# Dense part of V at 992 columns, every second block in three passes of rounded halves, five places for gathered rows

## The chip, the cores and the metric

One core of a Trainium2 chip runs the whole program in one launch. The metric is the device time of that core in microseconds (us), lower is better. The engines are PE (matmuls), ScalarE (ACT), VectorE (DVE), GpSimd (POOL, which here mostly issues gathers by index) and SyncE (SP, which issues plain loads and stores); 16 DMA engines serve all queues.

## The reference, cut to what matters

The program is one transformer layer for 256 tokens of width 2048: a mixer of several attentions, then a "PEER" layer of 16,384 experts. Only the last part of the second is touched. In it each token has 8 heads x 16 picked experts; each pick has a number `expert_idx`, made of two keys of 128 (`a * 128 + b`), and a weight `g * act`:

```
u = expert_u[expert_idx]                       # (tokens, 8, 16, 2048)
act = gelu(einsum('chkd,cd->chk', u, x))
vv = expert_v[expert_idx]
out = einsum('chk,chkd->cd', g * act, vv)      # sum over 128 picks of each token
```

All inputs and outputs are float32. The output is x plus the mixer plus this sum.

## The kernel before

**Two halves of V.** The sum over picks is made in two ways, split by columns. The first `V_ROW` = 1152 columns of each picked row are *gathered*: a pick (one of 256 = 2 tiles of 128 tokens x 128 picks; the kernel numbers them k) fetches one row of V for each of 128 tokens by an indirect DMA that POOL issues (`v_gather`, L671; 128 x 1152 floats, 576 KB), and its weighted row is added either by VectorE (`v_add`, L1597) or by PE with a diagonal of weights (`pick_add`, L2095). The last `V_DENSE` = 896 columns are *dense*: all 16,384 rows of V are read in 128 blocks of 128 rows (L598, SP's queue, 448 KB each), and PE multiplies each block with a 128 x 128 matrix of weights for each tile of tokens (`dense`, L2127). These weight matrices `dense_w` (tile 0 in `dense0`, tile 1 in `dense1`) are nearly all zeros, 128 picks for each token among 16,384; they are built from products of one-hot rows (`group`, L2118).

**The stages.** Up to some 440 us PE multiplies the mixer's inputs and outputs in three passes of rounded halves (L1692 to L1694): ScalarE copies a 1024-column piece into `split_hi` as F32R (L719), VectorE subtracts it to get `split_lo` (L1030), and hi x hi, hi x lo and lo x hi are added up. Then VectorE takes 256 products of gathered rows of U (L1549; POOL gathers them at L691), to about 1200 us; in this stage the first `V_BESIDE` = 36 rows of V are gathered and added by PE, into three places. Then comes the *seam* (1200 to 1280 us): 32 groups of four tokens build the weights of tile 1 (VectorE L1582, ScalarE L956 and L961, PE L2118), and 37 further rows of V are gathered and added, 21 by VectorE, 16 by PE, in the order `SEAM`. The last seam rows are k = 70 (VectorE), 71 and 72 (PE). Then comes the *dense stage*: PE does the 128 blocks, VectorE adds the remaining 183 rows (k from `V_AFTER` = 73 to 255).

**What sets the order in the dense stage.** Every queue runs in program order. SP issues the load of block a when block a - 4 is done on PE (`DENSE_PLACES` = 4, semaphore `dense_used`); the loads of blocks 1 to 3 wait for the last group of the seam, since the one-hot rows lie in their places. POOL issues gather k when the row that had its place (`v_place`, `v_before`) has been added; there are `V_PLACES` = 7 places, taken in turn. VectorE adds rows in the order of k, each addition waiting for the one before, and once, at k = 80, adds PE's share into tile 0 (`tile_out`, L1604). The last row is added in two halves (L1593), then the dense results are added from PSUM (L1665) as SP stores them (L602, L606). Nothing couples the rows to the blocks, except the DMA engines.

## Time and profile before

| | |
|---|---|
| median of 3 runs | 1690.85 us (1689.32 to 1690.89) |
| the profiled execution's own time | 1694.34 us |
| its span | 1692.5 us |
| PE busy | 1234.9 us (73%) |
| DVE busy | 1298.5 us (77%) |
| ACT busy | 460.9 us (27%) |
| POOL busy | 842.8 us (50%) |
| moved by DMA | 575.81 MB, mean 340 GB/s |

Busy times are of one profiled execution, in which PE's weight loads are counted apart. In rows of the profile `L671` is line 671 of the kernel, `xN` the number of instructions, and behind the bar stand busy us, mean ns of one, and the idle time of the engine before them with what ended it. A float32 matmul is recorded as two instructions. A matmul's recorded length contains its way through the array, so the distance of two starts, not the length, says how long PE is taken.

### The profile page before, as it was taken

The numbers are of one execution on the slowest core, as the hardware profiler recorded it, in microseconds if no ns is written. First come the engines' busy times: TensorE is split into PE (matmuls) and PEld (weight loads), VectorE is DVE, ScalarE is ACT, GpSimd is POOL, SyncE is SP. The second block draws the span as 40 slices with busy tenths as digits, with TensorE's granted clock in tenths as the row PEclk, the third lists the DMA queues.
The fourth block names the chain that finished last, engine by engine and source line by source line (L and its number), as shares of the span: only waits on it lengthen the run. The fifth ranks groups of instructions, "written<-read, shape, count | busy, mean of one in ns | idle before, by whom it ended". The sixth has DMA issues, their size and how long they took to land.

```text
span 1692.5 us, 14464 instructions
## 1 busy us (share of the span) xinstructions
PE 1234.9 (73%) x4812; PEld 839.8 (50%) x4812; DVE 1298.5 (77%) x1802; ACT 460.9 (27%) x1023; POOL 842.8 (50%) x546
## 2 busy tenths in 40 slices
PE   9999999999995554001344544454699999999993
PEld 7888887778984343000122322332365555555551
DVE  5554666466699999999999999999796665666667
ACT  5333443554200100000135565552381000000000
POOL 1000010000174888877888888888565443444444
PEclk9999999999997778555666676666699999999997
DMA  8886546348799999999999999999899999999998
GB/s 237 223 207 196 169 143 213 99 148 278 260 410 415 422 411 396 385 371 362 395 382 407 403 413 387 398 401 422 335 313 380 410 409 411 410 410 409 410 409 347
DMA packets 150230, 575.81 MB, mean 340 GB/s; under 512 B 15586, under 2 KB 28596, under 8 KB 117268
## 3 DMA queue, kind: packets, MB, share of 16 engines
q0 software_dynamic: 74384, 421.30, 62.6%
q1 hardware_dynamic: 75460, 152.82, 26.9%
q8 instruction: 35, 0.57, 0.1%
q10 hardware_dynamic: 320, 0.86, 0.1%
q14 instruction: 31, 0.25, 0.0%
HBM read 572.57 MB, written 2.36 MB: 340 GB/s over the span
## 4 chain that ended last, share of the span: by engine, by line
PE 30%; DVE 28%; DMA 24%; POOL 12%; issue 4%; ACT 2%; DVEq 0%; ACTq 0%; POOLq 0%
DMA v_rows<-in_peer_expert_v,pick_row 21%; DVE big L1549 10%; DVE more_rows L1549 8%; PE ps L1692 6%; PE ps L1694 6%; PE ps L1693 6%; POOL big L691 5%; PE ps L2095 4%; POOL more_rows L691 3%; DVE big L1597 3%; POOL v_rows L671 3%; DMA more_rows<-in_peer_expert_u,pick_row 2%; PE ps L2118 1%; DMA big<-in_peer_expert_u,pick_row 1%; DVE big L1574 1%
## 5 line engine op out<-in xcount | busy, mean ns | idle before, releaser
L671 POOL DMA_INDIRECT v_rows<-in_peer_expert_v,pick_row x256 | 307.8, 1202 | 271.7 <-DVE big L1597 234.9
L1597 DVE SCALAR_TENSOR_TENSOR big<-v_rows,pick_w,big 128x1152 f32<-128x1152 f32 x203 | 287.6, 1417 | 151.7 <-DMA v_rows<-in_peer_expert_v,pick_row 149.7
L2095 PE MATMUL ps<-v_rows,diag 128*128 128x512 f32 (+1 forms) x312 | 182.9, 746 | 269.5 <-DMA v_rows<-in_peer_expert_v,pick_row 169.8
L1549 DVE CUSTOM_DVE_ANT_0 big<-big 128x2048 f32<-128x2048 f32 x150 | 340.1, 2283 | 12.9 <-DMA big<-in_peer_expert_u,pick_row 12.5
L691 POOL DMA_INDIRECT big<-in_peer_expert_u,pick_row x150 | 288.8, 1925 | 65.6 <-issue 43.2
L2095 PEld LDWEIGHTS ps<-v_rows,diag 128*128 128x128 f32 x312 | 83.3, 285 | 368.2 <-issue 194.8
L691 POOL DMA_INDIRECT more_rows<-in_peer_expert_u,pick_row x106 | 222.7, 2101 | 75.3 <-issue 28.3
L1030 DVE TENSOR_TENSOR split_lo<-raw,split_hi 128x1024 fp32r<-128x1024 f32 x119 | 145.8, 1225 | 143.7 <-ACT split_hi L719 118.1
L1549 DVE CUSTOM_DVE_ANT_0 more_rows<-more_rows,big 128x2048 f32<-128x2048 f32 x106 | 240.8, 2284 | 11.0 <-DMA more_rows<-in_peer_expert_u,pick_row 11.0
L2127 PE MATMUL ps<-big,dense 128*128 128x512 f32 (+1 forms) x512 | 213.5, 539 | 0.3 <-DMA big<-in_peer_expert_v 0.3
L2127 PE MATMUL ps<-big 128*128 128x512 f32 (+1 forms) x512 | 213.4, 539 | 0.0
L1692 PE MATMUL ps<-split_hi,ht 128*128 128x512 f32 x476 | 189.3, 398 | 1.1 <-DVE split_lo L1080 0.9
L1694 PE MATMUL ps<-split_hi,ht 128*128 128x512 f32 x476 | 185.9, 390 | 0.0
L1693 PE MATMUL ps<-split_lo,ht 128*128 128x512 f32 x476 | 185.7, 390 | 0.0
L634 POOL TENSOR_TENSOR small<-small 128x2 f32<-128x2 f32 (+4 forms) x8 | 12.7, 1592 | 329.3 <-DVE small L1228 95.4
L2127 PEld LDWEIGHTS ps<-big,dense 128*128 128x128 f32 x512 | 97.1, 190 | 95.7 <-issue 61.2
L2127 PEld LDWEIGHTS ps<-big 128*128 128x128 f32 x512 | 97.3, 190 | 95.1 <-issue 61.2
L719 ACT ACTIVATE split_hi<-raw 128x1024 fp32r<-128x1024 f32 x97 | 102.9, 1060 | 148.9 <-PE ps L1694 148.1
L2118 PE MATMUL ps<-big 128*128 128x128 f32 x512 | 83.8, 324 | 50.5 <-ACT big L948 49.6
L1007 ACT ACTIVATE big<-ps 128x512 f32<-128x512 f32 x1 | 0.6, 598 | 388.0 <-PE ps L2127 388.0
L2118 PEld LDWEIGHTS ps<-big 128*128 128x128 f32 x512 | 78.5, 238 | 53.8 <-issue 50.9
L1692 PEld LDWEIGHTS ps<-split_hi,ht 128*128 128x128 f32 x476 | 89.4, 188 | 27.6 <-issue 3.2
(281 smaller groups left out, 1495.2 us busy)
## 6 DMA issues: line engine op xcount, KB each, us to landing
big<-in_peer_expert_v SPq DMA_DIRECT2D x128, 448.0 KB, 6.8
raw<-in_w_in SPq DMA_DIRECT2D x88, 512.0 KB, 3.7
raw<-in_w_out SPq DMA_DIRECT2D x32, 512.0 KB, 5.1
big<-in_peer_w_query SPq DMA_DIRECT2D x16, 512.0 KB, 6.5
raw<-in_peer_w_query SPq DMA_DIRECT2D x8, 512.0 KB, 7.6
spare<-in_peer_w_query SPq DMA_DIRECT2D x8, 512.0 KB, 8.3
v_rows<-in_peer_expert_v,pick_row POOLq DMA_INDIRECT x256, 14.2
big<-in_peer_expert_u,pick_row POOLq DMA_INDIRECT x150, 9.1
```

What stands on the lines that cost most here:

```text
L671: pool.indirect_dma_start(v_row(k), None, v_table, bass.IndirectOffsetOnAxis(pick_row[:, k:k + 1], 0)).then_inc(v_gathered[v_place(k)], 16)
L691: pool.indirect_dma_start(ring[u_place(m)], None, u_table, bass.IndirectOffsetOnAxis(pick_row[:, m:m + 1], 0)).then_inc(gathered[u_place(m ...
L719: act.activation(split_hi[:, s % SPLIT, :], raw[:, s % RAW, :], ACT.Copy).then_inc(hi_done, 1)
L1030: dve.tensor_tensor(split_lo[:, slot % SPLIT, 0:width], raw[:, slot, 0:width], split_hi[:, slot % SPLIT, 0:width].bitcast(F32), ALU.subtra ...
L1549: dve.tensor_tensor_reduce(row, row, XN[:, place_of(m // TOPK)[0], :], 1.0, 0.0, ALU.mult, ALU.add, pick_dot[:, m:m + 1]).then_inc(dotted, 1)
L1597: dve.scalar_tensor_tensor(out=v, in0=row, scalar=pick_w[:, k:k + 1], in1=v, op0=ALU.mult, op1=ALU.add).then_inc(added, 1)
L1692: pe.matmul(acc[t], h_h, w_h, start=k == 0, stop=False)
L1693: pe.matmul(acc[t], h_h, w_l, start=False, stop=False)
L1694: ins = pe.matmul(acc[t], h_l, w_h, start=False, stop=k == KC - 1)
L2095: ins = pe.matmul(psf[:, c:c + w], diag[:, j % DIAGS, :], row[:, c:c + w], start=k == 0, stop=j == pe_adds(PICKS) - 1)
L2118: pe.matmul(ps[:, 3 + i % 2, j * P:(j + 1) * P], hot[:, 1, :], hot[:, 0, :], start=True, stop=True).then_inc(token_made, 1)
L2127: ins = pe.matmul(psf[:, o:o + w], dense_w[t][:, a, :], row[:, c:c + w], start=a == 0, stop=a == NKEYS - 1, skip_group_check=True)
```

## The change

`V_ROW` becomes 1056 and so `V_DENSE` 992. Of the 128 blocks, those with an odd number from 5 on (62 of them, `SPLIT_BLOCKS`) are multiplied in three passes of rounded halves: hi x hi, hi x lo (the row's rest), lo (the weights' rest) x hi, where all blocks went in plain float32. For such a block a:

- ScalarE, once the block has landed and PE is done with block a - 4, copies the 992 columns into `dense_hi` (two places, laid over the last two of the seven places for gathered rows) and both 128 x 128 weight matrices into the slots of block a - 4, as F32R.
- VectorE subtracts: the row's rest goes into the block's own place, the weights' rest into their own slots. Its three subtractions stand in its program between additions of rows, at row 73 + (a - 2) * 183 // 128.
- PE waits for both before the block.

From row 73 on there are five places (`V_LATE`). ScalarE's first half waits until the rows of the seam are added. The store of tile 0's gathered columns, issued by ScalarE, is now behind block 63. Four waits on semaphores with names of their own became the engine's own step counter (`link`, `step`); the order of the instructions is the same.

```diff
-V_ROW = 1152
+V_ROW = 1056
 V_DENSE = D - V_ROW
 V_FIRST_PLACES, V_PLACES = 3, 7
+HI_PLACES, HI_BEHIND = 2, 4
+V_LATE = 5
+SPLIT_BLOCKS = [a for a in range(HI_BEHIND, NKEYS) if a % 2]
+SPLIT_AHEAD = 2
+OUT_0_AT = 63
+def split_after(n):
+    return [a for a in SPLIT_BLOCKS if max(0, a - SPLIT_AHEAD) * (PICKS - V_AFTER) // NKEYS == n]
 def v_place(k):
-    return k % V_FIRST_PLACES if k < V_BESIDE else (k - V_BESIDE) % V_PLACES
+    return k % V_FIRST_PLACES if k < V_BESIDE else (k - V_BESIDE) % V_PLACES if k < V_AFTER else (k - V_AFTER) % V_LATE
...
+        at_rows = at_big[0] - DENSE_PLACES * V_DENSE
+        dense_lo = nc.alloc_sbuf_tensor_at("dense_lo", [P, DENSE_PLACES, V_DENSE], F32R, offset=at_sbuf["big"] + 4 * at_rows)
+        split_w = [nc.alloc_sbuf_tensor_at(f"split_w{t}", [P, NKEYS, P], F32R, offset=at_sbuf["big"] + 4 * (A_PROJ if t else A_X1T)) for t in range(TT)]
+        dense_hi = nc.alloc_sbuf_tensor_at("dense_hi", [P, HI_PLACES, V_DENSE], F32R, offset=at_sbuf["ht"])
...
             group_out(1, GROUPS - 1)
-            act.wait_ge(sem("out_ready"), 1)
-            act.wait_ge(added, dve_adds(TILE_PICKS))
-            act.dma_start(out_rows[:, 0, 0:V_ROW], X[:, 0, 0:V_ROW]).then_inc(out_stored, 16)
+            act.wait_ge(group_moved, TT * GROUPS)
+            act.wait_ge(added, dve_adds(V_AFTER))
+            act.wait_ge(pe_added, pe_adds(V_AFTER))
+            for r, a in enumerate(SPLIT_BLOCKS):
+                act.wait_ge(dense_loaded[a % DENSE_PLACES], 16 * (a // DENSE_PLACES + 1))
+                act.wait_ge(dense_used, a - HI_BEHIND + 1)
+                act.activation(dense_hi[:, r % HI_PLACES, :], dense_rows[:, a % DENSE_PLACES, :], ACT.Copy).then_inc(dense_high, 1)
+                for t in range(TT):
+                    ins = act.activation(split_w[t][:, a - HI_BEHIND, :], dense_w[t][:, a, :], ACT.Copy)
+                ins.then_inc(dense_high, 1)
+                if a == OUT_0_AT:
...
+            def split_low(a):
+                r = SPLIT_BLOCKS.index(a)
+                dve.wait_ge(dense_high, 2 * r + 1)
+                dve.tensor_tensor(dense_lo[:, a % DENSE_PLACES, :], dense_rows[:, a % DENSE_PLACES, :],
+                                  dense_hi[:, r % HI_PLACES, :].bitcast(F32), ALU.subtract).then_inc(dense_split, 1)
+                dve.wait_ge(dense_high, 2 * r + 2)
+                for t in range(TT):
+                    ins = dve.tensor_tensor(split_w[t][:, a, :], dense_w[t][:, a, :], split_w[t][:, a - HI_BEHIND, :].bitcast(F32), ALU.subtract)
+                ins.then_inc(dense_split, 1)
             for k in range(V_AFTER, PICKS):
+                for a in split_after(k - V_AFTER):
+                    split_low(a)
...
             def dense(a):
+                if a in SPLIT_BLOCKS:
+                    r = SPLIT_BLOCKS.index(a)
+                    pe.wait_ge(dense_split, 2 * r + 2)
+                    hi, low = dense_hi[:, r % HI_PLACES, :], dense_lo[:, a % DENSE_PLACES, :]
+                    for t in range(TT):
+                        w_hi, w_low = split_w[t][:, a - HI_BEHIND, :], split_w[t][:, a, :]
+                        for w, row in ((w_hi, hi), (w_hi, low), (w_low, hi)):
+                            for c in range(0, V_DENSE, CHUNK):
+                                o, n = DENSE_AT[t] + c, min(CHUNK, V_DENSE - c)
+                                last = a == NKEYS - 1 and w is w_low
+                                ins = pe.matmul(psf[:, o:o + n], w, row[:, c:c + n], start=False, stop=last, skip_group_check=True)
+                    ins.then_inc(dense_used, 1)
+                    return
```

## Rows read from the trace of the kernel before

**Rows 1.** The page, part 2: busy share of the DMA engines, 40 slices.

```profile
DMA  8886546348799999999999999999899999999998
```

**Rows 2.** Stretches: PE, PEld, DVE, ACT, POOL, clock, DMA share, GB/s.

```profile
1300.00:1340.00 40.00, 40.00 (x108) 20.21 (x107) 24.83 (x18) 0.00 (x0) 16.49 (x18) 1.00 1.03 410
1660.00:1692.00 32.00, 6.43 (x18) 2.97 (x16) 26.81 (x21) 0.60 (x1) 14.88 (x12) 0.66 0.85 332
```

**Rows 3.** DMA view, 1300 to 1660 us: queues, and loads to landing.

```profile
q0 software_dynamic: 22404, 91.78, 63.3%
q1 hardware_dynamic: 17250, 55.00, 38.8%
...
big<-in_peer_expert_v SPq DMA_DIRECT2D x118, 448.0 KB, 6.8
v_rows<-in_peer_expert_v,pick_row POOLq DMA_INDIRECT x156, 14.4
```

**Rows 4.** Groups by shape, 1280 to 1692 us: VectorE's additions.

```profile
L1597 DVE SCALAR_TENSOR_TENSOR big<-v_rows,pick_w,big 128x1152 f32<-128x1152 f32 x180 | 255.3, 1418 | 149.9 <-DMA v_rows<-in_peer_expert_v,pick_row 148.1
...
L1593 DVE SCALAR_TENSOR_TENSOR big<-v_rows,pick_w,big 128x576 f32<-128x576 f32 x2 | 1.5, 814 | 0.1
...
L1665 DVE TENSOR_TENSOR big<-big,ps 128x896 f32<-128x896 f32 x1 | 1.1, 1078 | 0.0
...
L1665 DVE TENSOR_TENSOR big<-big,ps 128x384 f32<-128x384 f32 x1 | 0.5, 546 | 0.0
```

**Rows 5.** Timeline of VectorE, the end of the span.

```profile
1661.68 24.25 DVE L1597 SCALAR_TENSOR_TENSOR big<-v_rows,pick_w,big 128x1152 f32<-128x1152 f32 x16 [0.57 <-DMA v_rows<-in_peer_expert_v,pick_row]
1686.03 1.54 DVE L1593 SCALAR_TENSOR_TENSOR big<-v_rows,pick_w,big 128x576 f32<-128x576 f32 x2
```

**Rows 6.** Groups by shape, POOL, 770 to 1196 us: the gathers there.

```profile
L691 POOL DMA_INDIRECT big<-in_peer_expert_u,pick_row x94 | 187.9, 1999 | 31.4 <-issue 28.0 <-DVE pick_dot L1549 3.3
L691 POOL DMA_INDIRECT more_rows<-in_peer_expert_u,pick_row x48 | 97.7, 2035 | 14.6 <-issue 14.6
L671 POOL DMA_INDIRECT v_rows<-in_peer_expert_v,pick_row x37 | 84.2, 2274 | 11.3 <-issue 11.0 <-PE ps L2095 0.3
```

**Rows 7.** Timeline of PE: the last gathered row, the first block.

```profile
1278.00 2.17 PE L2095 MATMUL ps<-v_rows,diag 128*128 128x512 f32 x6 [0.17 <-ACT diag L917]
1280.01 1.67 PE L2127 MATMUL ps<-big,dense 128*128 128x512 f32 x4
```

**Rows 8.** Timeline of POOL there: the gather that PE releases.

```profile
1280.44 1.20 POOL L671 DMA_INDIRECT v_rows<-in_peer_expert_v,pick_row  x1 [0.32 <-PE ps L2095]
```

**Rows 9.** Timeline of PE, 1401 to 1405 us: two block starts.

```profile
1401.68 1.67 PE L2127 MATMUL ps<-big,dense 128*128 128x512 f32 x4
...
1404.68 1.67 PE L2127 MATMUL ps<-big,dense 128*128 128x512 f32 x4
```

**Rows 10.** Timeline of PE, 200 us: two rounded matmuls.

```profile
200.21 0.39 PE L1692 MATMUL ps<-split_hi,ht 128*128 128x512 f32 x1
200.44 0.39 PE L1693 MATMUL ps<-split_lo,ht 128*128 128x512 f32 x1
```

**Rows 11.** Groups by shape, 60 to 500 us: making rounded halves.

```profile
L1030 DVE TENSOR_TENSOR split_lo<-raw,split_hi 128x1024 fp32r<-128x1024 f32 x102 | 124.9, 1225 | 124.7 <-ACT split_hi L719 99.0 <-ACT split_hi L773 25.3
L719 ACT ACTIVATE split_hi<-raw 128x1024 fp32r<-128x1024 f32 x80 | 84.8, 1060 | 124.3 <-PE ps L1694 123.6 <-DMA raw<-in_w_out 0.8
```

**Rows 12.** Timeline of ACT, 1267 us: four copies of 128 columns.

```profile
1266.99 1.27 ACT L956 ACTIVATE big<-big,picks_t 128x128 f32<-128x128 f32 x4
```

**Rows 13.** Timeline of SP: the load behind that block start.

```profile
1401.87 0.33 SPq L598 DMA_DIRECT2D big<-in_peer_expert_v  x1
```

**Rows 14.** Line L598 over the whole span: issue to landing.

```profile
DMA to landing us min/median/max: 3.6/6.8/10.8
```

**Rows 15.** DMA view, 60 to 250 us: loads while DMA has room.

```profile
raw<-in_w_in SPq DMA_DIRECT2D x63, 512.0 KB, 3.6
```

**Rows 16.** DMA view, 770 to 1196 us: gathered rows of V.

```profile
v_rows<-in_peer_expert_v,pick_row POOLq DMA_INDIRECT x37, 8.7
```

More of the change, by code:

```diff
@@ L386, in layer @@
         assert A_XN <= at_big[0] - DENSE_PLACES * V_DENSE and at_big[0] <= A_X1T
+        at_rows = at_big[0] - DENSE_PLACES * V_DENSE
+        dense_lo = nc.alloc_sbuf_tensor_at("dense_lo", [P, DENSE_PLACES, V_DENSE], F32R, offset=at_sbuf["big"] + 4 * at_rows)
+        split_w = [nc.alloc_sbuf_tensor_at(f"split_w{t}", [P, NKEYS, P], F32R, offset=at_sbuf["big"] + 4 * (A_PROJ if t else A_X1T)) for t in range(TT)]
+        dense_hi = nc.alloc_sbuf_tensor_at("dense_hi", [P, HI_PLACES, V_DENSE], F32R, offset=at_sbuf["ht"])
+        assert HI_PLACES * V_DENSE + V_LATE * V_ROW <= OLD_HT * D
         hot0 = ring_rest.rearrange("p (s j n) -> p s j n", s=2, j=GROUP_TOKENS)
@@ L414, in layer @@
         query_used = sem("query_used")
+        dense_high, dense_split = sem("dense_high"), sem("dense_split")
         def query_name(n):
@@ L940, in hot_first @@
                     v = hot0[:, 1, j, :]
-                    act.activation(v, iota[:, :], ACT.Square, bias=picks_t[:, 1, token:token + 1], scale=-1.0).then_inc(sem("hot_squared"), 1)
-                    act.wait_ge(sem("hot_squared"), token + 1)
+                    link(act.activation(v, iota[:, :], ACT.Square, bias=picks_t[:, 1, token:token + 1], scale=-1.0))
                     act.activation(v, v, ACT.Relu, bias=1.0, scale=-1.0).then_inc(sem("hot_act"), 1)
@@ L1001, in _ @@
             group_out(1, GROUPS - 1)
-            act.wait_ge(sem("out_ready"), 1)
-            act.wait_ge(added, dve_adds(TILE_PICKS))
-            act.dma_start(out_rows[:, 0, 0:V_ROW], X[:, 0, 0:V_ROW]).then_inc(out_stored, 16)
+            act.wait_ge(group_moved, TT * GROUPS)
[9 more added lines that the diff above has]
+                if a == OUT_0_AT:
+                    act.wait_ge(sem("out_ready"), 1)
+                    act.wait_ge(added, dve_adds(TILE_PICKS))
+                    act.dma_start(out_rows[:, 0, 0:V_ROW], X[:, 0, 0:V_ROW]).then_inc(out_stored, 16)
             act.wait_ge(dense_used, NKEYS)
             v = slice(V_ROW, V_ROW + CHUNK)
-            act.activation(X[:, 1, v], ps[:, 6, :], ACT.Copy).then_inc(sem("dense_copied"), 1)
-            act.wait_ge(sem("dense_copied"), 1)
+            link(act.activation(X[:, 1, v], ps[:, 6, :], ACT.Copy))
             act.dma_start(out_rows[:, 1, v], X[:, 1, v]).then_inc(out_stored, 16)
@@ L1554, in head_weights @@
                 dve.wait_ge(sem("head_acted"), n + 1)
-                dve.wait_ge(sem("exp_inverse"), n + 1)
                 dve.scalar_tensor_tensor(out=pick_w[:, v], in0=pick_exp[:, v], scalar=exp_sum[:, n:n + 1], in1=pick_act[:, v],
@@ L1560, in weigh @@
                 dve.wait_ge(sem("head_exp"), n + 1)
-                dve.reciprocal(exp_sum[:, n:n + 1], exp_sum[:, n:n + 1]).then_inc(sem("exp_inverse"), 1)
+                link(dve.reciprocal(exp_sum[:, n:n + 1], exp_sum[:, n:n + 1]))
                 head_weights(n)
@@ L1625, in _ @@
             after()
-            dve.tensor_tensor(pick_exp[:, 0:TOPK], head_best, head_best[:, 0:1].broadcast_to([P, TOPK]), ALU.subtract).then_inc(sem("first_exp"), 1)
+            step(dve.tensor_tensor(pick_exp[:, 0:TOPK], head_best, head_best[:, 0:1].broadcast_to([P, TOPK]), ALU.subtract))
             first_rows(1, TOPK)
-            dve.wait_ge(sem("first_exp"), 1)
+            after()
             dve.wait_ge(sem("first_rows"), 2)
```

## The prediction

> **What bounds the kernel now.** I read the page's slices first: from about 460 us to the end the DMA engines stand at 8 or 9 tenths throughout [rows 1]. So I asked of each stage whether bytes set its length. In the dense stage they nearly do: between 1300 and 1340 us the share is 1.03 at 410 GB/s, but PE is also busy for 40.00 of 40 us, while VectorE has room (24.83) [rows 2]. The DMA view splits this into the gathers (63.3%) and the blocks (38.8%) [rows 3]: per MB, 0.69 and 0.71 points, so both cost by their bytes. A gathered row takes 14.4 us to land, a block 6.8 us. VectorE waits 148.1 us there for rows [rows 4]. PE is done by 1667 us (6.43 us busy from 1660 on [rows 2]); the last 16 whole rows go through VectorE back to back in 24.25 us, and the last row's halves begin at 1686.03, 6.5 us before the end of the span [rows 5]. Two things run side by side: PE with 128 blocks, and rows that wait for bytes and end some 20 us later.
>
> **The bytes.** A row shrinks by 96 x 4 x 128 = 49,152 bytes, a block grows by as much. 256 rows less 128 blocks give 6.3 MB less, 15.3 us at 410 GB/s. That is the ceiling. It has to be divided by stage.
>
> *Beside U* (36 rows, 1.77 MB, 4.4 us at 400 GB/s). POOL's gathers there fill the stretch: 187.9 + 97.7 + 84.2 us busy and 57.3 us of idle time around them make 427 of 426 us [rows 6]. A smaller row does not shorten an issue. Bounds 0 and 4.4 us saved; I take 1.5, nearer to POOL's rows.
>
> *Seam* (37 rows). VectorE, ScalarE and PE go in step here, and PE goes from its last pick_add straight into the first block [rows 7]. A row costs VectorE 0.1 us less, but PE still has the same number of matmuls and weight loads. I take nothing; bounds 0 and 21 x 0.1 = 2.1 us saved. PE then begins block 0 at 1278.5 instead of 1280.0.
>
> *The change to five places.* Gather 79 now waits for row 72, which PE frees, and is issued at 1280.44 [rows 8]. With five places that release belongs to gather 74. So at the start of the stage five rows fewer are under way, and 182 rows (98.4 MB) and 127 blocks (64.5 MB) are still to come: 162.9 MB or 397 us, where before 177 rows and 127 blocks made 162.7 MB. This is what the places cost: hardly a byte is saved in the dense stage itself. The first split is due behind row 76 and before block 5, some 17 us after the start, when these rows are there; so it delays nothing by itself.
>
> **PE.** Two starts of a block lie 3.00 us apart for 2 x 896 columns [rows 9]; 992 make 3.32. A rounded matmul of 512 columns takes 0.23 us from start to start [rows 10], one of 480 by the same rate 0.21: six of each are 2.64 us. A pair of one plain and one split block is 5.96 us, against 6.00 for two blocks before. PE alone gains 2 us in all.
>
> **VectorE and ScalarE.** The two lengths of the addition, 1418 and 814 ns [rows 4], give 1.05 ns a column, 1.32 us for 1056; back to back one takes 24.25 / 16 = 1.52 us, 0.10 more than its length [rows 5], so 1.42. Per pair of blocks there are 183 / 64 = 2.86 rows, 4.05 us. A split adds one subtraction of 992 columns: 1225 ns for 1024 columns [rows 11] and 1078 for 896 [rows 4] give 1.18 us; and two of 128, which the line through 1078 and 546 ns puts at 0.28 each, some 0.2 from start to start. Sum 5.65 us per pair. ScalarE's copy takes 1060 ns for 1024 columns [rows 11], 1.03 for 992, and its small ones 0.3 each [rows 12]; it was idle. The store on its queue moves, and nobody waits for it before the end. SP's and POOL's queues get no instruction more.
>
> **The chain that is new.** Before, a landed block was ready. Now the load of a split block is followed by ScalarE, VectorE and then PE, and the load still goes out only when block a - 4 is done. Steps from the start of block a - 3: SP issues 0.19 us later [rows 9, 13]; landing L; ScalarE 1.03; VectorE 1.18 and 0.45; four hand-overs at 0.1 us (my allowance, from the 0.10 above). That is L + 3.2 us. PE reaches block a after one plain, one split and one plain block, 9.3 us. L was 6.8 in the median, 3.6 to 10.8 overall [rows 14]. For 508 KB it lies between 3.6, the time of 512 KB where the DMA engines had room [rows 15], and 6.8 x 992 / 896 = 7.5. I take 6.8, since the competing rows shrink as the block grows. The chain then makes 10.0 us, 0.7 more than PE has. As two pairs T fit into the chain and the split block before it: T = (L + 3.2 + 2.64) / 2, that is 6.32 us at 6.8, under PE's 5.96 at 3.6, and 6.7 at 7.5.
>
> The DMA floor of a pair is two blocks and 2.86 rows, 2.56 MB at 410 GB/s: 6.25 us. VectorE's is 5.65, PE's 5.96. With four limits inside a tenth, and a landing time that scatters, the mean lies above the largest; I take **T = 6.4**. What is queued behind VectorE's wait for ScalarE is the next rows, and with them POOL's gathers; behind PE's wait are the next blocks and so SP's loads. So rows and blocks now march together.
>
> **The end.** After the last split five rows remain. The last row's halves start 4 x 1.42 us after the split; from there 6.6 us to the end, as before [rows 5] with 0.1 for wider results. From the last split 12.3 us, from PE's end 12.3 - 2.64 = 9.65 us.
>
> **Sum.** 1278.5 + 0.9 (x1 added on PE) + 4 x 3.32 + 62 x 6.4 + 9.65 = 1699.1 us of span, 6.6 above 1692.5. The profiled execution itself took 1694.34 and the median of the runs is 1690.85; I carry the difference over: **1697.4 us**. Waits that only changed their semaphore cost nothing: the same engine waits for the same instruction.
>
> **Rivals.** About 0.2% (3.4 us) can be told from no change.
>
> *A. Bytes decide after all (faster).* If landing falls to 6.6 us or less because fewer rows are in the queue, T is the DMA floor 6.25: 1689.8 of span. With all 4.4 us beside U it is 1686.9, with the 2.1 of the seam 1684.8. Times 1683 to 1688. For it: the share of 1.03, and 14.4 us of landing show a deep row queue that will be shallower. Against: PE and the chain sit right beside it.
>
> *B. Blocks cost more than their bytes.* A block's rows now begin 4224 bytes into a row of V, no multiple of 256; if fetches go by whole pieces of 256 they cost as 4096 bytes instead of 3968, 2 x 128 x 128 bytes per pair, 0.08 us: T = 6.33 at the least, 1694.8, so 1693.1 us. The rows seen so far (3584, 4608 bytes) are all multiples and cost alike per byte [rows 3], so no row speaks for or against. The Trainium skill (DMA: Bandwidth & Descriptors, How a descriptor splits into AXI transactions) says that a transfer which does not start on 256 bytes begins its first transaction at the boundary below and pays for the bytes before its start. By that rule the loss is the one just worked out; whether it holds here no row of before shows.
>
> *C. A late row holds up the splits (much slower).* VectorE is in order: a row that is not there stops the split behind it, and PE with it. The tightest is the row whose gather the first addition of a group releases: it is the third of the next group. Two pairs must hold its landing R, 1.5 us until its issue, its addition (1.42) and the split (1.6): T = (R + 4.5) / 2. At T = 6.4 this decides from R = 8.3 us. Rows of V took 8.7 us in the U stage [rows 16] and 14.4 in the dense stage with seven places [rows 3]; 8.7 gives T = 6.6, 9.1 gives 6.8. That is 1711 to 1724 of span, 1710 to 1722 us. For it: both measured landings lie over 8.3. Against: the five places themselves keep the queue short, and a shorter queue lands sooner.
>
> **How the numbers follow.** The forecast, T from 6.3 to 6.5 (1691 to 1704 us), 0.40, of which 0.12 lies within 0.2%. A 0.34, of which 0.28 is faster by over 0.2%. B 0.10, within. C 0.16, slower. Sums: faster 0.28, within 0.28, slower 0.44. The range 1682 to 1719 takes in A whole and most of C, and leaves out the worst rows of C and any gain beyond A's bounds.
>
> **What would show it.** Step by step: rounded matmuls at 0.23 us in the dense stage and PE's granted clock still 1.00; VectorE at about 0.88 of the stage; PE waiting for VectorE (the subtraction of the weights) before split blocks, about 0.4 us each, 27 us in all; VectorE's waits moving from gathered rows to ScalarE; ScalarE's waits on the block's landing; row landing at 7 to 8 us; the DMA share just under 1.03, at 400 GB/s. A is right if PE's waits come with a share of 1.03 and 410 GB/s; B if the share is full at fewer GB/s than 410; C if VectorE waits for rows and ScalarE has long been done. The forecast is wrong if landing of blocks is under 6.3 us or over 7.5, or if the U stage moves by more than 5 us.

## The result, and the profile after

| | before | after |
|---|---|---|
| median of the runs | 1691.01 us (20 runs) | 1699.94 us (20 runs) |
| the profiled execution | 1694.34 us, span 1692.5 | 1699.50 us, span 1697.6 |
| moved by DMA | 575.81 MB | 569.58 MB |

The changed kernel takes 1.0052 times as long, 95% interval 1.004 to 1.0064: 0.5% slower, some 8.8 us. The forecast of 1697.4 us lies 2.5 us under the median; the sign and the range were right. How far the terms were right is another matter: two of them were off in opposite directions and by luck nearly cancelled.

The start of the dense stage, on PE's timeline (start, length, engine, line, operation):

```profile
1269.35 2.10 PE L2132 MATMUL ps<-v_rows,diag 128*128 128x512 f32 x6 [0.17 <-ACT diag L933]
1271.28 1.91 PE L2177 MATMUL ps<-big,dense 128*128 128x512 f32 x4
...
1275.55 1.83 PE L2177 MATMUL ps<-big,dense 128*128 128x512 f32 x4
1277.21 1.83 PE L2177 MATMUL ps<-big 128*128 128x512 f32 x4
1278.87 1.83 PE L2177 MATMUL ps<-big,dense 128*128 128x512 f32 x4
...
1289.01 0.71 PE L2169 MATMUL ps<-dense_hi,split_w 128*128 128x512 f32 x2
```

These answer to [rows 7]. PE begins at 1271.28 instead of 1280.01, a plain block takes 3.32 us (1275.55 to 1278.87), and the first split block begins at 1289.01, with no wait. From there the stage loses what it had won. Eighteen pairs of blocks further on, still PE's timeline, the start of two split blocks and the plain one between them:

```profile
1403.95 0.72 PE L2169 MATMUL ps<-dense_hi,split_w 128*128 128x512 f32 x2
...
1406.74 1.82 PE L2177 MATMUL ps<-big,dense 128*128 128x512 f32 x4
...
1410.51 0.71 PE L2169 MATMUL ps<-dense_hi,split_w 128*128 128x512 f32 x2 [0.28 <-DVE split_w L1689]
```

The pair takes 6.56 us here. From the first split block (1289.01) to the last (1685.19) are 61 pairs of 6.495 us on average; PE's own work is some 6.04 us (run 4 below, in which PE hardly waits). The stretch that answers to the first of [rows 2], and the DMA view that answers to [rows 3]:

```profile
1300.00:1340.00 40.00, 38.31 (x124) 22.51 (x122) 31.81 (x37) 8.57 (x18) 26.13 (x19) 1.00 1.01 389
```

```profile
q0 software_dynamic: 22654, 85.05, 60.0%
q1 hardware_dynamic: 15999, 56.45, 40.4%
...
big<-in_peer_expert_v SPq DMA_DIRECT2D x111, 496.0 KB, 6.8
v_rows<-in_peer_expert_v,pick_row POOLq DMA_INDIRECT x159, 8.6
```

The granted clock stays at 1.00, and the DMA share at 1.01; but that share now goes with 389 GB/s in the stretch and 395 from 1300 to 1660 us, where before 1.03 went with 410. Rows land in 8.6 us, not 14.4, blocks in 6.8 as before. Who waits, from 1280 us to the end (waiter, what it waited for, us in total, times, longest):

```profile
POOL v_rows L687 <- DVE big L1621: 133.8, 101, 5.1
...
PEld ps L2169 <- DVE split_w L1689: 55.5, 56, 2.7
DVE big L1621 <- DMA v_rows<-in_peer_expert_v,pick_row: 55.3, 63, 5.9
DVE dense_lo L1685 <- ACT dense_hi L1023: 25.2, 20, 4.1
...
PE ps L2169 <- DVE split_w L1689: 15.1, 23, 1.9
```

Before, VectorE's waits for rows, 148.1 us of them [rows 4], never held up PE. Now 55.3 us are left, but VectorE's order carries the splits, and PE waits for VectorE. Only 20 of the 62 splits found ScalarE not yet done; the other 42 began as soon as the rows in front of them had been added. In VectorE's timeline 39 of these 42 have a wait for a row since the split before, and in front of their blocks PE's pair is 6.57 us on average; the three splits without any wait have 6.15, and the 14 that waited for ScalarE alone 6.34. What the new work costs by itself, in groups by shape:

```profile
L1621 DVE SCALAR_TENSOR_TENSOR big<-v_rows,pick_w,big 128x1056 f32<-128x1056 f32 x181 | 238.4, 1317 | 61.8 <-DMA v_rows<-in_peer_expert_v,pick_row 55.3 <-DVE big L1621 0.5
...
L1685 DVE TENSOR_TENSOR dense_lo<-big,dense_hi 128x992 fp32r<-128x992 f32 x62 | 73.6, 1187 | 25.4 <-ACT dense_hi L1023 25.2
...
L1023 ACT ACTIVATE dense_hi<-big 128x992 fp32r<-128x992 f32 x62 | 63.9, 1030 | 325.5 <-DMA big<-in_peer_expert_v 325.5
...
L1689 DVE TENSOR_TENSOR split_w<-dense,split_w 128x128 fp32r<-128x128 f32 x62 | 17.6, 285 | 0.0
```

All four lengths are those of the prediction (1.32, 1.18, 1.03 and 0.28 us), within 0.01. And the end, VectorE's timeline, which answers to [rows 5]:

```profile
1685.05 5.58 DVE L1621 SCALAR_TENSOR_TENSOR big<-v_rows,pick_w,big 128x1056 f32<-128x1056 f32 x4
1691.09 1.45 DVE L1617 SCALAR_TENSOR_TENSOR big<-v_rows,pick_w,big 128x528 f32<-128x528 f32 x2 [0.46 <-DVE big L1621]
```

Four whole rows and two halves after the last split, as counted.

### The profile page after: what moved, and what is told of

Its sections match the earlier page's. It is cut to its first block, busy times and chain, and to the rows that moved or that the text cites. A ratio compares the mean times of both kernels' runs of the same rounds, so it can differ in the third digit from the quotient of the medians.

```text
span 1697.6 us, 15395 instructions
## 1 busy us (share of the span) xinstructions
PE 1244.6 (73%) x5060; PEld 881.1 (52%) x5060; DVE 1369.1 (81%) x1988; ACT 549.7 (32%) x1209; POOL 915.7 (54%) x546
## 2 busy tenths in 40 slices
DMA packets 150236, 569.58 MB, mean 336 GB/s; under 512 B 15586, under 2 KB 28596, under 8 KB 117268
## 4 chain that ended last, share of the span: by engine, by line
PE 33%; DVE 23%; DMA 18%; POOL 16%; issue 7%; ACT 3%; DVEq 0%; ACTq 0%; POOLq 0%
DMA v_rows<-in_peer_expert_v,pick_row 10%; POOL big L707 8%; DVE more_rows L1574 7%; DVE big L1574 7%; PE ps L1729 6%; PE ps L1731 6%; PE ps L1730 6%; POOL more_rows L707 5%; DMA big<-in_peer_expert_v 4%; POOL v_rows L687 3%; DVE big L1621 3%; PE ps L2132 3%; DMA more_rows<-in_peer_expert_u,pick_row 3%; PE ps L2169 3%; PE ps L2177 2%
## 5 line engine op out<-in xcount | busy, mean ns | idle before, releaser
L687 POOL DMA_INDIRECT v_rows<-in_peer_expert_v,pick_row x256 | 377.9, 1476 | 203.3 <-DVE big L1621 140.9
L2132 PE MATMUL ps<-v_rows,diag 128*128 128x512 f32 (+1 forms) x312 | 170.2, 702 | 267.6 <-DMA v_rows<-in_peer_expert_v,pick_row 169.5
L1621 DVE SCALAR_TENSOR_TENSOR big<-v_rows,pick_w,big 128x1056 f32<-128x1056 f32 x203 | 267.2, 1316 | 67.7 <-DMA v_rows<-in_peer_expert_v,pick_row 61.2
L707 POOL DMA_INDIRECT more_rows<-in_peer_expert_u,pick_row x106 | 227.4, 2146 | 81.2 <-issue 28.0
L1023 ACT ACTIVATE dense_hi<-big 128x992 fp32r<-128x992 f32 x62 | 63.9, 1030 | 325.5 <-DMA big<-in_peer_expert_v 325.5
L2169 PE MATMUL ps<-dense_hi,split_w 128*128 128x512 f32 x496 | 150.8, 405 | 15.9 <-DVE split_w L1689 15.1
L2169 PEld LDWEIGHTS ps<-dense_hi,split_w 128*128 128x128 f32 x496 | 89.4, 188 | 72.3 <-DVE split_w L1689 55.5
L2177 PE MATMUL ps<-big,dense 128*128 128x512 f32 (+1 forms) x264 | 121.1, 581 | 0.0
L2177 PE MATMUL ps<-big 128*128 128x512 f32 (+1 forms) x264 | 120.6, 579 | 0.0
L2155 PEld LDWEIGHTS ps<-big 128*128 128x128 f32 x512 | 77.6, 234 | 55.5 <-issue 52.6
```

Of the source, the lines that this page charges most:

```text
L687: pool.indirect_dma_start(v_row(k), None, v_table, bass.IndirectOffsetOnAxis(pick_row[:, k:k + 1], 0)).then_inc(v_gathered[v_place(k)], 16)
L707: pool.indirect_dma_start(ring[u_place(m)], None, u_table, bass.IndirectOffsetOnAxis(pick_row[:, m:m + 1], 0)).then_inc(gathered[u_place(m ...
L1621: dve.scalar_tensor_tensor(out=v, in0=row, scalar=pick_w[:, k:k + 1], in1=v, op0=ALU.mult, op1=ALU.add).then_inc(added, 1)
L2132: ins = pe.matmul(psf[:, c:c + w], diag[:, j % DIAGS, :], row[:, c:c + w], start=k == 0, stop=j == pe_adds(PICKS) - 1)
L2155: pe.matmul(ps[:, 3 + i % 2, j * P:(j + 1) * P], hot[:, 1, :], hot[:, 0, :], start=True, stop=True).then_inc(token_made, 1)
L2169: ins = pe.matmul(psf[:, o:o + n], w, row[:, c:c + n], start=False, stop=last, skip_group_check=True)
```

## The experiments

Every run was timed in 5 rounds beside the kernel before on the same chip; ratios are of medians to that kernel, with 95% intervals. The pair time T (one plain and one split block) is worked out for each from the starts of the first and the last split block on PE's timeline, over 61 pairs. It comes from one profiled execution, and executions of one kernel differ by some us: 3 us of span are 0.05 us of T. Differences in T below that say nothing.

**1. The widths alone.** The kernel before with

```diff
-V_ROW = 1152
+V_ROW = 1056
```

> The kernel before with the widths 1056 and 992 alone: all 128 blocks in plain float32, seven places for gathered rows, no work of ScalarE or VectorE on blocks. Both theories: the start of the dense stage moves from 1280.0 to about 1271.5 us as in the changed kernel (1271.28), since smaller rows are all that differs there; if instead it stays near 1278 to 1280, the 8.7 us came from elsewhere. The dense stage is then PE's alone: 0.9 + 128 x 3.33 = 427 us, so PE ends near 1699 us, and 5 us of results and stores make a span near 1704, 11 us over the kernel before and 6 over the changed one. VectorE waits for rows about as before, and rows are all added before PE ends.

Measured: 1709.49 us, ratio 1.0112 (1.0096 to 1.0129), span 1706.5. PE starts the stage at 1273.45 and works 360.00 of 360 us. VectorE, at the end:

```profile
1644.56 1.45 DVE L1593 SCALAR_TENSOR_TENSOR big<-v_rows,pick_w,big 128x528 f32<-128x528 f32 x2 [1.05 <-DMA v_rows<-in_peer_expert_v,pick_row]
1701.18 1.75 DVE L1665 TENSOR_TENSOR big<-big,ps 128x992 f32<-128x992 f32 x2 [55.17 <-PE ps L2127]
```

The last row is added 55 us before PE is done. So without splits this width is PE's alone, and at this width splits and five places together do save: the whole change is 6 parts in 1000 better than this. The start of the stage was as expected, but see what all runs together say of it below.

**2. Five places alone.** The kernel before with

```diff
-    return k % V_FIRST_PLACES if k < V_BESIDE else (k - V_BESIDE) % V_PLACES
+    return k % V_FIRST_PLACES if k < V_BESIDE else (k - V_BESIDE) % V_PLACES if k < V_AFTER else (k - V_AFTER) % 5
```

> The kernel before with five instead of seven places for gathered rows from row 73 on, nothing else. Theory 'chain' (the split blocks' way from landing over ScalarE and VectorE sets the pace, places cost little): landing of rows falls from 14.4 to about 10 us, the DMA share stays at 1.03 and 410 GB/s, the span grows by 0 to 3 us for the drained start. Theory 'late rows' (five places cannot keep the queue full): the share falls under 1.0, 400 GB/s or less, and the span grows by 8 us or more.

Measured: 1702.33 us, ratio 1.0063 (1.0048 to 1.0079), span 1701.8. Neither theory as put. Landing falls to 9.7 us and the share stays at 1.03 with 409 GB/s, as "chain" has it; the span grows by 9.3 us, as "late rows" has it. The time goes at the start (VectorE's timeline):

```profile
1279.72 1.42 DVE L1597 SCALAR_TENSOR_TENSOR big<-v_rows,pick_w,big 128x1152 f32<-128x1152 f32 x1 [4.67 <-DMA v_rows<-in_peer_expert_v,pick_row]
1286.03 1.42 DVE L1597 SCALAR_TENSOR_TENSOR big<-v_rows,pick_w,big 128x1152 f32<-128x1152 f32 x1 [4.89 <-DMA v_rows<-in_peer_expert_v,pick_row]
```

From 1260 to 1300 us the DMA engines move 313 GB/s instead of 361. Five rows not fetched in the seam are 2.95 MB, 7.2 us at 410 GB/s. The prediction had counted these five rows, as the reason why hardly a byte is saved in the dense stage; this run shows what they cost where nothing else changes.

**3. The old widths with splits and five places.** The changed kernel with

```diff
-V_ROW = 1056
+V_ROW = 1152
```

> The changed kernel at the old widths of 1152 and 896 columns: splits and five places stay. The dense stage starts near 1280 us again. PE's pair of blocks is 3.00 + 2.4 = 5.4 us, and the chain with the shorter subtraction and matmuls is (6.8 + 3.1 + 2.4) / 2 = 6.15 us. Theory 'bytes': a pair moves 2.605 MB, 6.35 us at 410 GB/s, so the pair takes 6.35 to 6.45 and the span is about 1698 to 1704. Theory 'late rows': five places hold larger rows that land later, the pair takes 6.6 or more, the span is over 1712. Theory 'chain': a pair at 6.15 to 6.3, PE's waits shrink against the changed kernel.

Measured: 1701.63 us, ratio 1.007 (1.0055 to 1.0085), span 1697.9, T = 6.473 us. PE's pair is 0.6 us shorter here than in the changed kernel by the expectation's sum, the chain's limit on T 0.17 us lower (6.15 for 6.32), and the pair of blocks takes the same time within scatter. So PE's length does not set the pace; of the chain's 0.17 us that is less sure. From 1300 to 1660 us VectorE is busy for 301.69 of 360 us and waits for rows (39.7 us) more than for ScalarE (14.6). Of the three expectations "bytes" comes nearest in the number, with 402 GB/s, but the DMA engines moved more in runs 4 and 12 (417 and 420). And against the run with five places alone the splits cost nothing that can be told (1.007 and 1.0063).

**4. Without VectorE's part.** The changed kernel with

```diff
-                for a in split_after(k - V_AFTER):
-                    split_low(a)
...
-                    pe.wait_ge(dense_split, 2 * r + 2)
-                    hi, low = dense_hi[:, r % HI_PLACES, :], dense_lo[:, a % DENSE_PLACES, :]
+                    pe.wait_ge(dense_high, 2 * r + 2)
+                    hi = low = dense_hi[:, r % HI_PLACES, :]
...
-                        w_hi, w_low = split_w[t][:, a - HI_BEHIND, :], split_w[t][:, a, :]
-                        for w, row in ((w_hi, hi), (w_hi, low), (w_low, hi)):
+                        w_hi = w_low = split_w[t][:, a - HI_BEHIND, :]
+                        for w, row in ((w_hi, hi), (w_hi, hi), (w_hi, hi)):
```

> The changed kernel without VectorE's subtractions; PE waits for ScalarE's rounded copies alone and multiplies hi x hi three times in place of the three different products (the lower halves of the split blocks are left out of the result). PE's work is the same. If VectorE's part of the way (its 1.6 us and the rows it stands behind) sets the pace, the pair of blocks falls from 6.49 us to the DMA floor, 6.25, or to PE's 5.97, and PE's waits for a split block nearly vanish: the stage ends 12 to 25 us sooner, span 1675 to 1686. If the landing of blocks or the DMA engines set the pace, a pair stays at 6.4 or more, span 1692 or more, and PE waits for ScalarE instead.

Measured: 1682.43 us, ratio 0.9952 (0.9933 to 0.9971), span 1678.7, 18.9 us under the changed kernel's. PE is busy for 359.93 of 360 us, so T is PE's own: 6.04 us over the 61 pairs, 0.07 more than the sum of 5.97. The DMA view from 1300 to 1660 us:

```profile
q0 software_dynamic: 23883, 89.70, 61.2%
q1 hardware_dynamic: 16945, 59.75, 40.7%
```

That is 150.20 MB, 417 GB/s, from the same widths, the same five places, and the same way over ScalarE. VectorE's part in the blocks is what costs. Neither the bytes nor the landing of blocks by itself (6.6 us) held the changed kernel at 6.49. The edit takes three things away at once: VectorE's 1.5 us of work per split, its place in the chain from landing to PE, and the tie between rows and blocks. Runs 6 and 11 ask which.

**5 and 6. 1024 columns, with five and with six places.** The changed kernel with `V_ROW = 1024`, and in the second run also

```diff
-V_LATE = 5
+V_LATE = 6
```

> The changed kernel with both parts 1024 columns wide, five places. Rows and blocks are then whole multiples of 256 bytes and start on one. Theory 'boundary': the share of the DMA engines per MB goes back to the 0.69 to 0.705 points of before (0.706 and 0.716 in the changed kernel between 1300 and 1660 us), and with 2.1 MB less the stage is 5 to 10 us shorter as far as DMA sets it. Theory 'bytes only': the share per MB stays where it is. PE's pair grows to 3.42 + 2.72 = 6.14 us, the chain to (6.8 + 3.3 + 2.72) / 2 = 6.4. If the chain sets the pace, the span stays within 4 us of 1697.6.

> As the run with 1024 columns, but six places for gathered rows from row 73 on, which just fit. Only the places differ between the two. Theory 'late rows' (a row that has not landed holds VectorE, the split behind it and so PE): six places give a row 2.2 us more, VectorE's waits for rows (55 us in the changed kernel) fall by half or more and the span is 8 us or more under that with five. Theory 'chain': the two agree within 3 us, and VectorE's waits move from rows to ScalarE.

Measured with five: 1707.55 us, ratio 1.0087 (1.0065 to 1.011), span 1706.4, T = 6.683. With six: 1702.49 us, ratio 1.0076 (1.0054 to 1.0098), span 1699.1, T = 6.560. VectorE's waits from 1270 us on, first with five, then with six:

```profile
DVE big L1621 <- DMA v_rows<-in_peer_expert_v,pick_row: 57.1, 55, 6.2
DVE dense_lo L1685 <- ACT dense_hi L1023: 39.3, 28, 3.1
```

```profile
DVE dense_lo L1685 <- ACT dense_hi L1023: 72.8, 54, 3.6
DVE big L1621 <- DMA v_rows<-in_peer_expert_v,pick_row: 10.7, 3, 4.9
```

This pair is the clearest on the waits. One place more and the waits for rows go, but most of the time stays: the splits now wait for ScalarE 54 times instead of 28, and T falls by 0.12 us only. The spans differ by 7.3 us, near the 8 of "late rows", while the waits move as "chain" has it. With a landing of 7.0 us, the chain of the prediction gives (7.0 + 3.3 + 2.72) / 2 = 6.51 us for six places; 6.56 was measured. So there are two limits close together: late rows while there are five places, the chain behind it. By the times alone the two kernels can't be told apart: their intervals overlap.

The question of the boundary: per MB the DMA share was 0.724 and 0.723 points with 1024 columns and five places (58.6% for 80.89 MB, 40.7% for 56.26 MB), although everything starts on 256 bytes. With 1056 and 992 it was 0.706 and 0.716 in the changed kernel and 0.682 and 0.681 in run 4. The share is near 1 in all of them, so per MB it only says how many MB were moved, and it shows nothing of the boundary. The stage got longer, not 5 to 10 us shorter.

**7. Splits one block earlier in VectorE's program.**

```diff
-SPLIT_AHEAD = 2
+SPLIT_AHEAD = 3
```

> The changed kernel with each split one block (1.4 rows) earlier in VectorE's program (ahead by 3 instead of 2). Theory 'late rows': with fewer rows in front of it a split is reached before ScalarE is done, VectorE's waits move from rows to ScalarE, and PE's waits shrink until the chain at 6.3 us binds: 0 to 10 us faster than 1697.6. Theory 'chain': VectorE stands longer before ScalarE and the rows fall behind, PE keeps its pace: within 3 us, or some us slower by the rows left at the end (1.4 rows more, 2 us).

Measured: 1705.73 us, ratio 1.0082 (1.0062 to 1.0102), span 1713.1, T = 6.619. The median is 5.8 us over the changed kernel's, more than either theory had, though the intervals (1.0052 there, 1.004 to 1.0064) still touch. The profiled execution is the slowest of the six, 9 us over their median, so its T says little. Nor do its waits: VectorE waited 62.5 us for rows (60.6 in the changed kernel, both from 1270 us on) and 32.3 us for ScalarE, for 25.2, but one wait before the first split block makes all the difference, against 2.70 us at that place in the changed kernel:

```profile
1293.88 1.19 DVE L1685 TENSOR_TENSOR dense_lo<-big,dense_hi 128x992 fp32r<-128x992 f32 x1 [7.87 <-ACT dense_hi L1023]
```

So the earlier place gains nothing; why it loses is not shown. The expectation of run 10 builds on these 32 us and the 6.62, and with them on this one wait and a slow execution.

**8. Every fourth block.**

```diff
-SPLIT_BLOCKS = [a for a in range(HI_BEHIND, NKEYS) if a % 2]
+SPLIT_BLOCKS = [a for a in range(HI_BEHIND, NKEYS) if a % 4 == 1]
...
-OUT_0_AT = 63
+OUT_0_AT = 65
```

> The changed kernel with every fourth block split (5, 9, 13, ...; 31 in place of 62). PE takes 2.64 + 3 x 3.33 = 12.6 us for four blocks, 3.16 a block, against 3.24 measured in the changed kernel; the three plain blocks before a split are 10 us, as long as the chain, so PE hardly waits. VectorE has half the splits. If chain or late rows set the pace of the changed kernel: a stage of 13.3 + 31 x 12.6 = 404 us and a tail of 6 to 10, span near 1682 to 1688, faster than both kernels. If the DMA engines set it (2.56 MB a pair at 395 GB/s as measured, 6.49 us): no faster than the changed kernel, span near 1697.

Measured: 1697.84 us, ratio 1.0044 (1.0028 to 1.006), span 1694.2. Four blocks take 12.87 us, 0.27 more than PE's 12.6, and PE works 356.77 of 360 us; so PE nearly sets the pace, as expected. But 0.27 us for each of 31 is 8 us, and PE is done only at 1686.4 us, near 1678 by the expectation's sum. VectorE ends the rows at 1689 us, later still, with 94 us of waits for them, so a faster PE alone would not have given the expected 1682 to 1688 us. Why the rows are late here, with half the splits, was not taken apart; the five places are a guess.

**9. The start refilled.** Rows 73 to 76 keep seven places, row 77 takes that of 71:

```diff
-    return k % V_FIRST_PLACES if k < V_BESIDE else (k - V_BESIDE) % V_PLACES if k < V_AFTER else (k - V_AFTER) % V_LATE
+    return k % V_FIRST_PLACES if k < V_BESIDE else (k - V_BESIDE) % V_PLACES if k < V_AFTER + 4 else (k - V_AFTER - 4) % V_LATE
...
-            act.wait_ge(added, dve_adds(V_AFTER))
+            act.wait_ge(added, dve_adds(V_AFTER + 4))
```

> The changed kernel with seven places for rows 73 to 76 as well, and five from row 77 on, counted anew so that row 77 takes the place of 71; ScalarE's first half waits for row 76 too. The gathers of 73 to 76 then go out in the seam as before the change, instead of waiting for rows 71 and 72. Theory 'start' (the 10 us that five places alone cost come from the DMA engines standing idle around the start of the dense stage): VectorE's two waits of 5 to 6 us for rows there vanish and the DMA share from 1260 to 1300 us goes back from 0.81 to 0.95 or more. Under 'lockstep' (rows and blocks march together from the first split on, at PE's and VectorE's pace) most of that head start is not turned into time, as PE starts and paces the blocks just the same: 0 to 3 us off the span. Under 'bytes decide' 5 rows or 6 to 7 us come off.

Measured: 1700.31 us, ratio 1.006 (1.0037 to 1.0082), span 1695.4, T = 6.456. VectorE's timeline after the seam:

```profile
1270.70 2.74 DVE L1621 SCALAR_TENSOR_TENSOR big<-v_rows,pick_w,big 128x1056 f32<-128x1056 f32 x2 [0.80 <-DMA v_rows<-in_peer_expert_v,pick_row]
1287.54 1.19 DVE L1685 TENSOR_TENSOR dense_lo<-big,dense_hi 128x992 fp32r<-128x992 f32 x1 [14.09 <-ACT dense_hi L1023]
```

The two waits for rows are gone, and VectorE stands for 14.09 us before the first block that is to be split. The rows' head start is waited away there, and the time is as before the edit: "lockstep", not "bytes". The DMA share from 1260 to 1300 us, expected at 0.95 by "start", came only to 0.85: VectorE, waiting, freed no places.

**10. Splits one block later.** `SPLIT_AHEAD = 1`.

> The changed kernel with each split one block (1.4 rows) later in VectorE's program (ahead by 1 instead of 2). With the splits earlier the pair of blocks grew from 6.49 to 6.62 us, and VectorE's waits for ScalarE from 25 to 32 us. If what costs is that VectorE stands before ScalarE while landed rows keep their places, the later split takes 15 us or more off these waits, the pair falls to 6.3 to 6.45, and three rows instead of five remain behind the last split: 4 to 12 us off the span. If instead late rows in front of the split cost most, VectorE waits longer for rows, PE waits longer for VectorE, and the pair grows to 6.6 or more.

Measured: 1700.18 us, ratio 1.0045 (1.0027 to 1.0064), span 1700.1, T = 6.523. Neither theory's T. Waits for ScalarE fell by 4 us only, waits for rows grew by 4. No gain that can be told from none: of the three places tried none is better than the one chosen in the change.

**11. The weights' halves first.** On both engines the weights' work stands before the row's; shown for VectorE:

```diff
-                dve.wait_ge(dense_high, 2 * r + 1)
-                dve.tensor_tensor(dense_lo[:, a % DENSE_PLACES, :], dense_rows[:, a % DENSE_PLACES, :],
-                                  dense_hi[:, r % HI_PLACES, :].bitcast(F32), ALU.subtract).then_inc(dense_split, 1)
-                dve.wait_ge(dense_high, 2 * r + 2)
+                dve.wait_ge(dense_high, 2 * r + 1)
                 for t in range(TT):
                     ins = dve.tensor_tensor(split_w[t][:, a, :], dense_w[t][:, a, :], split_w[t][:, a - HI_BEHIND, :].bitcast(F32), ALU.subtract)
                 ins.then_inc(dense_split, 1)
+                dve.wait_ge(dense_high, 2 * r + 2)
+                dve.tensor_tensor(dense_lo[:, a % DENSE_PLACES, :], dense_rows[:, a % DENSE_PLACES, :],
+                                  dense_hi[:, r % HI_PLACES, :].bitcast(F32), ALU.subtract).then_inc(dense_split, 1)
```

> The changed kernel with the weights' halves made before the row's, on ScalarE and on VectorE. The weights need no landing, so VectorE's two subtractions (0.45 us) and their hand-over leave the way from landing to PE. No engine has more or less to do. Theory 'chain' (landing, ScalarE, VectorE, PE): a pair is (L + 2.75 + 2.64) / 2 instead of (L + 3.2 + 2.64) / 2, 0.2 us less for 62 pairs, 8 to 14 us off the span. Theory 'VectorE's order' (rows that are not there hold up the splits): the split starts when the rows in front are added, its length is the same, and the span stays within 3 us.

Measured: 1698.55 us, ratio 1.0041 (1.0024 to 1.0058), span 1698.6, T = 6.477, 0.02 us less than in the changed kernel. The chain is 0.45 us shorter by the lengths of its steps, and the pair is shorter by 0.02 us where 0.2 was expected (12 us of span, well outside scatter). With five places the chain is not what sets the pace. That leaves VectorE's order with its late rows, as the waits by split above have it.

**12. A width between the two, with nothing else.** The kernel before with

```diff
-V_ROW = 1152
+V_ROW = 1120
```

> The kernel before with the widths 1120 and 928 alone: no split blocks, seven places. At 1152 PE ended its blocks some 20 us before the last row, at 1056 (the run with the widths alone) VectorE was done with the rows 55 us before PE. A line between the two puts the balance a third of the way down, at 1120. PE: 0.9 + 128 x 3.00 x 928 / 896 = 399 us from a start at 1275 to 1279, so it ends at 1674 to 1678; the last row's halves begin 41 / 3 = 14 us sooner than at 1152, near 1672. Span 1680 to 1685, 8 to 12 us under the kernel before and under every split version: ratio 0.993 to 0.996. If rows and blocks slow each other more than the two ends show, it stays within 3 us of the kernel before.

Measured: 1682.39 us, ratio 0.9943 (0.9929 to 0.9956), span 1681.9. VectorE's timeline at the end, and the stretch 1300 to 1340 us:

```profile
1670.02 1.51 DVE L1593 SCALAR_TENSOR_TENSOR big<-v_rows,pick_w,big 128x560 f32<-128x560 f32 x2 [0.83 <-DMA v_rows<-in_peer_expert_v,pick_row]
1676.71 1.62 DVE L1665 TENSOR_TENSOR big<-big,ps 128x928 f32<-128x928 f32 x2 [5.18 <-PE ps L2127]
```

```profile
1300.00:1340.00 40.00, 40.00 (x104) 19.45 (x103) 25.00 (x19) 0.00 (x0) 16.86 (x18) 1.00 1.03 419
```

Span and ratio are as expected. The rows end some 5 us before PE, where before they ended 20 us behind it. One changed number makes a kernel that is faster than both.

## Why the prediction was right, and where it was not

**The start of the stage was mis-sized.** Predicted 1278.5, measured 1271.28 us. The step was "beside U 1.5, seam nothing". In the two profiled executions VectorE's last product of U ends 3.5 us earlier (1200.8 and 1197.3), inside the bounds given, and the seam is shorter by 5.3 us (79.3 and 74.0), where the prediction took nothing and set 2.1 as the bound. But part of the 7 us is scatter from one execution to the next: with 1152 columns the stage began at 1280.0, 1278.9 and 1273.2 us (before, runs 2 and 3), with 1056 between 1271.3 and 1277.6 in eight kernels, 1273.6 on average, at 1024 at 1268.7 and 1268.2. By these means the smaller rows are worth 3.8 us ahead of the stage, not 1.5, and the one profiled execution of before began late. Runs 2 and 3 have five places besides, so a part of this may be the places' (fewer rows fetched in the seam); with seven places there is one execution at each width, 1280.0 at 1152, 1275.4 at 1120 and 1273.5 at 1056.

**The work was sized right.** The plain block (3.32 us), ScalarE's and VectorE's lengths and the tail (12.4 us from the last split block's start on PE to the end, 12.3 predicted from the split) all came out. So did the clock, and the landing of blocks. A split block takes PE 2.72 us (run 4's 6.04 less 3.32), not 2.64; PE's own pair is then 6.04, not 5.96, which moves nothing, as T lies above both.

**The pair came out at 6.495, not 6.4.** 61 pairs make 5.8 us of that. With the start, 7.2 us the other way, the two errors nearly cancel by luck, and the span is 1697.6 against 1699.1 predicted. In the medians the loss is larger, 8.9 us for a predicted 6.5.

**The step that failed is the reason for T.** The prediction said that the chain (landing, ScalarE, VectorE, PE) makes 6.32 us and scatter the rest, and kept the late row as rival C with 0.16. Run 11 took 0.45 us out of the chain and gained 0.02 us per pair where the chain would have given 0.2. Run 3 shortened chain and PE's work and kept T. 42 of the 62 splits had not waited for ScalarE, and 39 of these had waited for rows. The prediction's own sign for C (VectorE waits for rows and ScalarE has long been done) came for these 42; its sign for the forecast, waits moving from rows to ScalarE, came for 20. VectorE was busy for 0.80 of the stage, not 0.88. C's own formula, (R + 4.5) / 2, gives 6.55 us at the measured landing of 8.6 us, for 6.495 measured; its threshold of 8.3 us was passed, though not by as much as C had priced. For run 5, with a landing of 8.9 us, the formula gives 6.70 for 6.683 measured, for run 3, also 8.9, it gives 6.70 for only 6.473; it is good to 0.2 us at best. So the mechanism was C's at nearly the forecast's price, and that the price came out is luck. The chain is not refuted as a limit: with six places (run 6) VectorE waits for ScalarE before 54 splits, and its formula gives 6.51 for 6.56. It is the second limit, at 1024 columns 0.12 us behind the first. That would explain why no single edit of order or place (runs 6, 7, 9, 10, 11) gained more than its interval; it is an argument, as no run relieved both limits and kept the splits.

**What both have in common was tried directly.** Without VectorE's part (run 4) the stage runs at PE's pace and the kernel is 0.5% faster than before. The prediction had this in one sentence ("rows and blocks now march together") and did not price it as such.

**Rival A.** The DMA floor was put at 6.25 us by 410 GB/s. It was lower: run 4 moved 417, run 12 419 to 420 GB/s. A failed not by the floor but because VectorE's part kept the kernel from coming down to it.

**Rival B.** No cost of the boundary was seen. In run 4, with rows that start 4224 bytes into a row of V, the DMA engines moved a pair of blocks and its rows in 6.04 us, at 417 GB/s, so B's 6.33 was no limit. Run 12's blocks start 4480 bytes into a row, no multiple of 256 either, and it moved 420 GB/s, more than before with all starts on 256 (410). The Trainium skill's rule (DMA: Bandwidth & Descriptors, How a descriptor splits into AXI transactions) makes 128 bytes more for each 3968 of a block, an estimate of 3%; these runs don't show it. Nor do they refute it: the engines were not at a known limit, and whether the fetches themselves are longer was not measured by itself.

**Five places.** The prediction counted what they cost in bytes, five rows more to fetch in the dense stage, and gave them no time of their own, as T is set by the pairs. At the old widths they cost 0.6% by themselves (run 2). In the changed kernel the drained start is hidden, since the blocks pace the rows: refilling it gained nothing (run 9). So the step was right for the changed kernel.

**Left open.** Which part of the 0.45 us per pair between run 4 and the changed kernel is VectorE's being busy (1.5 us per split), which the order of its instructions, and which the longer issues of gathers that the last section shows: 0.46 us more per row, shared by five places, would by an estimate be 0.09 us per row and 0.26 us per pair of 2.86 rows, if the places set the pace of the rows. Moving the subtractions to another engine, or a second set of places, was not tried; the places would not fit beside this width.

## What to carry to other kernels

When one engine serves two streams in program order, its load is not what to look at (80% here) but what each stream does while the other is waited for: while it stands for one, it frees no buffers of the other (the 14 us of run 9), and the two then go at one pace, which here was slower than either would have had alone. Before adding such a coupling to relieve an engine, look at how far apart two uncoupled streams end: here PE ended some 20 us ahead of the rows, and moving 32 columns from one to the other was worth more than three passes, 62 splits and all their waits. And in a stage with a fixed number of buffers, count how many are in flight at its start: in run 2 the rate within the stage was as before (409 GB/s), and the time went at the start.

## What the runs showed of the hardware

A DMA share near 1 did not mean that the engines had no room. From 1300 to 1660 us the same share of 1.00 to 1.03 went with 383 GB/s (run 5), 395 (after), 410 (before), 417 (run 4) and 420 (run 12).

GpSimd's issue of one gather took 943 ns before (1152 columns), 958 in run 4, and 1417 in the changed kernel (both 1056 columns) (1300 to 1640 us, first run 4, then the changed kernel):

```profile
L687 POOL DMA_INDIRECT v_rows<-in_peer_expert_v,pick_row x156 | 149.5, 958 | 189.8 <-DVE big L1621 185.3 <-issue 4.5
```

```profile
L687 POOL DMA_INDIRECT v_rows<-in_peer_expert_v,pick_row x150 | 212.5, 1417 | 128.6 <-DVE big L1621 108.5 <-issue 20.2
```

The two kernels differ in VectorE's part (218.29 and 289.50 busy of 360 us) and in what PE reads and waits for. All 80 of the 150 issues that took over 1.2 us in the changed kernel, 1.80 us on average, began while VectorE was busy without a break; the 34 issues beside which VectorE stood idle for a while took 1.12 us at the most. On average an issue is longer by 0.46 us, on top of the landing of each row. The Trainium skill (SBUF — State Buffer, SBUF: two separate sides) says that VectorE and GpSimd share one pair of SBUF ports, which an instruction of VectorE with two SBUF inputs holds for its whole length against a GpSimd operation that reads SBUF. The longer issues agree with that in direction; that issuing a gather is such an operation, and that it is this lock, no run here shows.
